# The first projection of a two-layer encoder trunk: the order of modulation and projection in the opening

## The chip, the cores and the metric

The kernel runs on one core of a Trainium2 chip, as one launch. The time is the device time of that launch, in microseconds (us). A core has a matrix engine (TensorE, PE in the rows; its weight loads are PEld), a vector engine (VectorE, DVE), an activation engine (ScalarE, ACT), GpSimd (POOL) and a queue engine (SyncE, SP). Each has its own list of instructions, and they wait for each other by semaphores. TensorE writes into eight banks of accumulator memory: `proj0`, `proj1`, `z0` to `z3`, `obank`, `misc`. Everything else lies in on-chip memory of 128 partitions, filled by DMA.

## The reference

The input x has 512 rows of 1024 values, c has 1024 values. What bears on the change is the start of layer 0:

```python
cond = jax.nn.silu(c)
mod = cond @ ada_w[l] + ada_b[l]
sh1, sc1, g1, sh2, sc2, g2 = jnp.split(mod, 6, axis=-1)
h = modulate(rms_norm(x, norm_mix_g[l]), sh1, sc1)     # h * (1 + scale) + shift
proj = h @ w_in                                        # 1024 x 2304 in layer 0
sq, sk, sv, wq, wk, wv = jnp.split(proj, cuts, axis=-1)
```

The projections feed stick-breaking attention (8 heads: logits, a log-sigmoid, a suffix sum over the keys, weights, values) and a sliding-window attention with sinks. Then come an output projection, a gated feed-forward net with a convolution, a second layer with a gated linear recurrence, and a last norm.

## The kernel before

A row of 1024 values is eight blocks of 128 (`DC = 8`). The activations lie transposed, block by block: `hT_hi[:, dc, :]` is block dc of the modulated input for all 512 rows. Each product is made of three matmuls in a faster number format: the value is split in a high part (`hi`, a copy by ScalarE) and the rest (`lo`, a subtraction by VectorE), and hi times hi, lo times hi and hi times lo are summed. A unit is one block of 128 output columns: 8 blocks x 3 = 24 matmuls of 512 columns. Its weights come into `w_raw`, ScalarE makes `w_hi` (`split`, L654), VectorE `w_lo` (L1068).

The list `STEPS0` orders layer 0 on all engines: `Q` is the opening group of four units, `u` a unit, `A` the logits of a head, `B` its suffix sums, `C` the values of two heads, `T` a transpose of values, `L` a window head. The lists of the engines are written out by hand in this order; nothing reorders them.

The opening, before the first `A`: SyncE loads x, then half of the shift and scale columns of `ada_w` (8 pieces of 512 KB, L512), the weights of the four units for the first four blocks (L522), the other half of the columns, the other weights. ScalarE sums the squares of x, scales its rows by the inverse root (L726), TensorE transposes them (L1867), ScalarE copies them as `x_hat` (L730). The rows of x are transposed without the factor too, for the residual `xT` (L1796, L752). VectorE multiplies each piece of the columns by its value of `cond` and adds it up over the 8 pieces (`first_block`, L1165, L1168). TensorE sums that over the partitions with a column of ones (`first_sums`), VectorE adds the bias and makes `scale_g` (`first_columns`, L1175, L1179). ScalarE makes the high part of the modulated block with scale and shift in one instruction (L738), and the block itself (L745); VectorE the low part (L1196). TensorE computes the four units SQ, SK, SV and WK for the first half of the blocks (`quad(0)`), and, after the second half of the columns, for the rest (`quad(1)`). Between its pieces of work it runs matmuls whose result nobody reads (`keep_clock`).

After `Q`, `A` 0 starts. `flip` (L1278) copies queries and keys to the other half of the partitions. For each head VectorE makes four sums (L1360) and four low parts (L1366), for which `B` waits. `ada_blocks` sums further modulation columns (L1208, L1211), `clear_queries` writes zeros (L1284, L1285).

## Time and profile before

| what | value |
|---|---|
| median of 3 runs | 1299.79 us (1299.79 to 1300.24) |
| the profiled execution, its own time | 1300.57 us |
| its span | 1298.8 us |
| TensorE busy | 1262.1 us, 97% |
| VectorE busy | 818.4 us, 63% |
| ScalarE busy | 554.8 us, 43% |
| chain that ended last | PE 88%, DVE 5%, queue of SP 2%, ACT 2%, DMA 1% |

The span is what the trace covers; the rest of the execution's own time lies around it. In the rows a line such as L1168 is a line of the kernel; an idle time in square brackets stands with what ended it. Where several matmuls stand in one row, the time runs from the start of the first to the end of the last. A matmul of full precision makes two records.

### The profile page before, as it was taken

What the parts mean: (1) busy time and instruction counts of PE and PEld (TensorE: products, weight loads), DVE (VectorE), ACT (ScalarE), POOL (GpSimd) and SP (SyncE); (2) the same over time, 40 slices, a digit from 0 to 9 for tenths busy, and PEclk for the clock granted to TensorE, in tenths of its full rate; (3) what the DMA queues carried; (4) which work ended last, traced back from release to release, by engine and by line L of the source; (5) the groups of instructions that cost most, each with busy time, mean ns of one, the idle gap of its engine ahead of it and who ended that gap; (6) DMA issues with size and microseconds to landing.
All of it is one profiled execution on the core that took longest, in us unless ns stands there. A gap on an engine that the chain in (4) does not pass through costs nothing.

```text
span 1298.8 us, 18991 instructions
## 1 busy us (share of the span) xinstructions
PE 1262.1 (97%) x7071; PEld 1021.7 (79%) x7071; DVE 818.4 (63%) x1191; ACT 554.8 (43%) x837; POOL 46.8 (4%) x92
## 2 busy tenths in 40 slices
PE   6999998999999999999999999999999999999997
PEld 5777777868888888878778888888688888888786
DVE  5776667676666666556787887776855555552423
ACT  7665556343333333121356655653433333331212
POOL 1000000000000000001000000001000000000000
PEclk9999999999999999999999999999999999999999
DMA  9644520535445454556513222226233333332232
GB/s 331 196 130 146 163 81 2 163 97 162 145 142 146 134 154 145 172 160 226 184 55 94 66 82 74 78 78 210 66 102 96 96 95 97 97 97 97 92 103 81
DMA packets 190074, 160.09 MB, mean 123 GB/s; under 512 B 5271, under 2 KB 163176, under 8 KB 190018
## 3 DMA queue, kind: packets, MB, share of 16 engines
q1 hardware_dynamic: 177696, 116.34, 29.7%
q0 software_dynamic: 11776, 42.29, 10.8%
q8 instruction: 38, 0.62, 0.2%
q10 hardware_dynamic: 546, 0.69, 0.1%
q14 instruction: 18, 0.15, 0.0%
HBM read 157.20 MB, written 2.10 MB: 123 GB/s over the span
## 4 chain that ended last, share of the span: by engine, by line
PE 88%; DVE 5%; SPq 2%; ACT 2%; issue 1%; DMA 1%; DVEq 0%; ACTq 0%
PE proj L1684 62%; PE z L1684 21%; PE obank L1684 3%; PE misc L1684 1%; SPq L512 1%; SPq L522 1%; DVE normed L1106 1%; DVE hT_lo L1112 1%; ACT w_hi L654 1%; DMA w_raw<-ab_w_in 1%; DVE w_lo L1068 0%; DVE xT L1491 0%; PE z L2244 0%; ACT hT_hi L686 0%; PE misc L1957 0%
## 5 line engine op out<-in xcount | busy, mean ns | idle before, releaser
L1684 PE MATMUL proj<-hT_hi,w_hi 128*128 128x512 f32 x1112 | 439.6, 396 | 1.1 <-ACT hT_hi L686 0.9
L1684 PE MATMUL proj<-hT_lo,w_hi 128*128 128x512 f32 x1112 | 434.6, 391 | 2.9 <-DVE hT_lo L1112 2.9
L1068 DVE TENSOR_TENSOR w_lo<-w_raw,w_hi 128x1024 fp32r<-128x1024 f32 x189 | 231.1, 1224 | 321.4 <-ACT w_hi L654 321.3
L1684 PE MATMUL proj<-hT_hi,w_lo 128*128 128x512 f32 x1112 | 433.2, 390 | 0.0
L654 ACT ACTIVATE w_hi<-w_raw 128x1024 fp32r<-128x1024 f32 x191 | 201.9, 1058 | 404.0 <-PE proj L1684 230.9
L1684 PEld LDWEIGHTS proj<-hT_lo,w_hi 128*128 128x128 f32 x1112 | 208.8, 188 | 52.4 <-DVE hT_lo L1112 9.3
L1684 PEld LDWEIGHTS proj<-hT_hi,w_hi 128*128 128x128 f32 x1112 | 208.8, 188 | 50.3 <-issue 8.7
L1684 PEld LDWEIGHTS proj<-hT_hi,w_lo 128*128 128x128 f32 x1112 | 208.7, 188 | 44.2
L1684 PE MATMUL z<-gated_hi,w_hi 128*128 (+1 forms) x264 | 103.6, 392 | 2.7 <-DVE xT L1491 2.7
L1684 PE MATMUL z<-gated_hi,w_lo 128*128 (+1 forms) x264 | 103.1, 390 | 0.0
L1684 PE MATMUL z<-gated_lo,w_hi 128*128 (+1 forms) x264 | 103.0, 390 | 0.0
L1211 DVE SCALAR_TENSOR_TENSOR ada_sum<-ada_raw,cond,ada_sum 128x1024 f32<-128x1024 f32 x70 | 89.6, 1280 | 2.8 <-DMA ada_raw<-ada_w 0.7
L906 ACT ACTIVATE square<-square,small 128x512 f32<-128x512 f32 x44 | 31.9, 724 | 133.8 <-DVE square L1454 133.8
L600 POOL DMA_DIRECT2D ada_raw<-ada_w x80 | 42.2, 528 | 843.4 <-DVE ada_sum L1211 439.2
L1684 PEld LDWEIGHTS z<-gated_hi,w_hi 128*128 128x128 f32 x264 | 49.6, 188 | 13.7 <-DVE xT L1491 3.1
L1684 PEld LDWEIGHTS z<-gated_hi,w_lo 128*128 128x128 f32 x264 | 49.7, 188 | 10.5
L1684 PEld LDWEIGHTS z<-gated_lo,w_hi 128*128 128x128 f32 x264 | 49.7, 188 | 10.0
L1461 DVE TENSOR_TENSOR h<-proj,square 128x512 f32<-128x512 f32 x44 | 30.4, 691 | 20.9 <-ACT square L906 20.0
L672 ACT ACTIVATE square<-xT 128x512 f32<-128x512 f32 x28 | 17.7, 632 | 51.5 <-DVE xT L1416 31.4
L1454 DVE SCALAR_TENSOR_TENSOR square<-normed,small,square 128x512 f32<-128x512 f32 x44 | 33.1, 752 | 6.6 <-DVE square L1450 5.8
L1684 PE MATMUL proj<-gated_hi,w_hi 128*128 (+1 forms) x88 | 35.2, 400 | 0.6 <-DVE w_lo L1068 0.6
L1450 DVE SCALAR_TENSOR_TENSOR square<-normed,small,square 128x512 f32<-128x512 f32 x44 | 33.1, 751 | 3.9 <-DVE square L1447 0.2
(342 smaller groups left out, 1485.5 us busy)
## 6 DMA issues: line engine op xcount, KB each, us to landing
ada_raw<-ada_w POOLq DMA_DIRECT2D x80, 512.0 KB, 4.2
w_raw<-ffn_w_gate SPq DMA_DIRECT2D x44, 512.0 KB, 3.8
w_raw<-ffn_w_up SPq DMA_DIRECT2D x44, 512.0 KB, 3.8
w_raw<-ffn_w_down SPq DMA_DIRECT2D x44, 512.0 KB, 3.3
w_raw<-hg_w_in SPq DMA_DIRECT2D x32, 512.0 KB, 4.1
ada_first<-ada_w SPq DMA_DIRECT2D x16, 512.0 KB, 11.0
w_raw<-ab_w_in SPq DMA_DIRECT2D x14, 512.0 KB, 4.0
w_raw<-ab_w_out SPq DMA_DIRECT2D x8, 512.0 KB, 4.2
```

The lines of the kernel that those rows point to most:

```text
L512: sp.dma_start(ada_first[:, DC * (1 - h) + k, :].rearrange("p (g n) -> p g n", g=2), src).then_inc(ada_first_in[h][k], 16)
L522: sp.dma_start(w_raw[:, p, i * 512:(i + 1) * 512].rearrange("p (k n) -> p k n", k=HALVES0), columns(rows, P * QUAD[2 * p + i])).then_inc(r ...
L600: pool.dma_start(ada_raw[:, m % ADA_SLOTS, :], ada_w[layer].rearrange("(p k) n -> p k n", k=DC)[:, k, which * D:(which + 1) * D]).then_inc ...
L654: nc.scalar.activation(dst, w_raw[:, slot, :], ACT.Copy).then_inc(hi_done, 1)
L672: nc.scalar.activation(dst, xT[:, dc, :], ACT.Square).then_inc(sq_done, 1)
L906: nc.scalar.activation(square[:, 1, :], square[:, 0, :], ACT.Gelu_apprx_tanh, bias=conv_col(layer, 3, f)).then_inc(gelu_done, 1)
L1068: nc.vector.tensor_tensor(w_lo[:, slot, :], w_raw[:, slot, :], w_hi[:, slot, :].bitcast(F32), ALU.subtract).then_inc(lo_done, 1)
L1211: nc.vector.scalar_tensor_tensor(out=acc, in0=raw, scalar=scale, in1=acc, op0=ALU.mult, op1=ALU.add).then_inc(ada_used, 1)
L1450: nc.vector.scalar_tensor_tensor(out=square[:, 0, :], in0=normed[:, 0, 1:1 + SEQ], scalar=conv_col(layer, 1, f), in1=square[:, 0, :], op0= ...
L1454: nc.vector.scalar_tensor_tensor(out=square[:, 0, :], in0=normed[:, 0, 2:2 + SEQ], scalar=conv_col(layer, 2, f), in1=square[:, 0, :], op0= ...
L1461: nc.vector.tensor_tensor(h32[:, 0, :], proj[1][:], square[:, 1, :], ALU.mult).then_inc(gp_done, 1)
L1684: return nc.tensor.matmul(dst, weights_ap, moving, start=start, stop=stop, skip_group_check=True)
```

## The change

The opening is put in another order. SyncE loads the weights of the four units in four pieces (a piece holds two blocks, for all four units) and between them the scale columns, for blocks 0 and 1, 2 and 3, 4 to 7; after them the shift columns, the weights of two single units, and the tables. The four units are SQ, SQ+1, SK and SK+1; SV and WK follow as single units after `A` 0.

The factors of the scale are summed by TensorE alone: per block and piece four matmuls with a weight of 128x32 and one moving column, `cond` (`scale_products`). The inverse root is spread over the partitions by TensorE (`diag`), and VectorE multiplies xT by it (`hat`). The four units are computed over x_hat times scale, without the shift. The shift is summed as before, by VectorE over 8 pieces (`shift_sums`); its part of the four units is a number per output column, made by 128 small matmuls from the raw weights (`quad_bias_of`) and added where the banks are copied out. The modulated input with the shift, which all later units need, is then made anew: `shifted_high` on ScalarE, `shifted_value` and `shifted_low` on VectorE, eight blocks. GpSimd makes the low weights of the units 4 and 5.

On VectorE, before, from the last block of the first half to the last one ahead of `A` 0 (`hT_lo` is a low part of the input, `ada_sum` the sums over the pieces, `quad_w` low weights):

```order
L1196 TENSOR_TENSOR hT_lo<-normed,hT_hi 128x512
L1168 SCALAR_TENSOR_TENSOR ada_sum<-ada_first,cond,ada_sum 128x1024 x5
L1074 TENSOR_TENSOR quad_w<-w_raw,quad_w 128x1024
L1175 TENSOR_TENSOR mod<-misc,small 128x2x4
L1179 SCALAR_TENSOR_TENSOR scale_g<-mod,small 128x4
L1190 TENSOR_SCALAR normed<-x_hat,scale_g,mod 128x512
L1196 TENSOR_TENSOR hT_lo<-normed,hT_hi 128x512
L1074 TENSOR_TENSOR quad_w<-w_raw,quad_w 128x1024
L1196 TENSOR_TENSOR hT_lo<-normed,hT_hi 128x512 x3
```

The same engine with the change, from the low part of block 4 to the first block with the shift:

```order
L1262 SCALAR_TENSOR_TENSOR hT_lo<-x_turn,scale_g,hT_hi 128x512
L1204 TENSOR_SCALAR ada_sum<-x_nat,cond 128x1024
L1207 SCALAR_TENSOR_TENSOR ada_sum<-x_nat,cond,ada_sum 128x1024
L1262 SCALAR_TENSOR_TENSOR hT_lo<-x_turn,scale_g,hT_hi 128x512
L1207 SCALAR_TENSOR_TENSOR ada_sum<-x_nat,cond,ada_sum 128x1024 x2
L1262 SCALAR_TENSOR_TENSOR hT_lo<-x_turn,scale_g,hT_hi 128x512
L1207 SCALAR_TENSOR_TENSOR ada_sum<-shift_low,cond,ada_sum 128x1024 x2
L1262 SCALAR_TENSOR_TENSOR hT_lo<-x_turn,scale_g,hT_hi 128x512
L1207 SCALAR_TENSOR_TENSOR ada_sum<-shift_low,cond,ada_sum 128x1024
L1207 SCALAR_TENSOR_TENSOR ada_sum<-ada_sum,cond 128x1024
L1235 TENSOR_TENSOR mod<-misc,small 128x8
L1269 TENSOR_SCALAR normed<-x_turn,scale_g,mod 128x512
```

The eight sums of the first half are gone, those that are left lie between the low parts of blocks 4 to 7, and the remade input begins behind them.

On VectorE around `A` 0, before (`k_sw` are window keys, `oT` and `h` the copies of `flip`):

```order
L1068 TENSOR_TENSOR w_lo<-w_raw,w_hi 128x1024 x2
L1328 COPY k_sw<-obank 64x512 x4
L1278 COPY oT<-q_sb 64x512 x2
L1278 COPY h<-k_sb 64x512 x2
L1360 SCALAR_TENSOR_TENSOR soft_a<-z,soft_a 128x128
```

With the change, from the copy of the second queries on (`normed` is a block with the shift):

```order
L1352 TENSOR_SCALAR q_sb<-proj,c_now 128x512
L1269 TENSOR_SCALAR normed<-x_turn,scale_g,mod 128x512
L1275 TENSOR_TENSOR hT_lo<-normed,hT_hi 128x512
L1269 TENSOR_SCALAR normed<-x_turn,scale_g,mod 128x512
L1275 TENSOR_TENSOR hT_lo<-normed,hT_hi 128x512
L1269 TENSOR_SCALAR normed<-x_turn,scale_g,mod 128x512
L1275 TENSOR_TENSOR hT_lo<-normed,hT_hi 128x512
L1358 TENSOR_SCALAR k_sb<-obank,c_now 128x512
L1269 TENSOR_SCALAR normed<-x_turn,scale_g,mod 128x512
L1275 TENSOR_TENSOR hT_lo<-normed,hT_hi 128x512
L1269 TENSOR_SCALAR normed<-x_turn,scale_g,mod 128x512
```

Seven more pairs of this kind and two copies stand ahead of the first `flip`; the window keys come after the first head's low parts.

On TensorE with the change, the columns of the scale (`cond,scale_...`) inside the blocks 1 and 3 of the four units:

```order
L1782 MATMUL z<-hT_hi,w_hi 128x512
L1782 MATMUL proj<-hT_hi,w_hi 128x512 x2
L1782 MATMUL obank<-hT_hi,w_hi 128x512
L1782 MATMUL z<-hT_hi,w_lo 128x512
L1782 MATMUL proj<-hT_hi,w_lo 128x512 x2
L1782 MATMUL obank<-hT_hi,w_lo 128x512
L1782 MATMUL z<-cond,scale_early 32x1 x64
L1782 MATMUL z<-hT_lo,w_hi 128x512
L1782 MATMUL proj<-hT_lo,w_hi 128x512 x2
...
L1782 MATMUL z<-cond,scale_late 32x1 x128
L1782 MATMUL z<-hT_lo,w_hi 128x512
L1782 MATMUL proj<-hT_lo,w_hi 128x512 x2
```

Block 1 ends behind 64 small matmuls and block 3 behind 128; before, 32 stood ahead of each half. The core of the diff:

```diff
-QUAD = [SQ, SK, SV, WK]
+QUAD = [SQ, SQ + 1, SK, SK + 1]
 STEPS0 = [
-    ("Q", 0), ("A", 0), ("T", 0), ("u", SQ + 1), ("B", 0), ("u", SK + 1),
+    ("Q", 0), ("A", 0), ("u", SV), ("u", WK), ("B", 0), ("T", 0),
...
+EARLY = len(QUAD) + 2
+PIECES = 4
+SCALES = [(0, 2, 0), (1, 2, 2), (2, 4, 4)]
...
+            def scale_load(i):
+                at, n, dc = SCALES[i]
+                for j in range(DC // 2):
+                    sp.dma_start(scale_raw[i][:, 2 * j:2 * j + 2, :],
+                                 first_ada[:, 2 * j:2 * j + 2, 1, dc * P:(dc + n) * P]
+                                 ).then_inc(scale_in[i][j * len(scale_in[i]) // 4], 16)
+
+            def shift_load(k):
+                sp.dma_start(shift_raw[k], first_ada[:, k, 0, :]).then_inc(shift_in[k // 2], 16)
...
             quad_load(0)
...
+            scale_load(0)
             quad_load(1)
+            scale_load(1)
+            quad_load(2)
+            scale_load(2)
+            quad_load(3)
+            sp.wait_ge(xt_full, DC)
+            for k in range(4):
+                shift_load(k)
+            unit_load(4)
             sp.dma_start(table2, tables[:, 2 * P:9 * P]).then_inc(bands_in, 16)
...
+            for k in range(4, DC):
+                shift_load(k)
+            unit_load(5)
+
...
+            def early_split(u):
+                pool.wait_ge(hi_done, u + 1)
+                nc.gpsimd.tensor_tensor(w_lo[:, u % 2, :], w_raw[:, u % 2, :], w_hi[:, u % 2, :].bitcast(F32),
+                                        ALU.subtract).then_inc(early_low, 1)
+
+            for u in range(len(QUAD), EARLY):
+                early_split(u)
+
+            pool.wait_ge(misc_full, MISC_AT["bias1"] + 1)
...
+            def first_high(dc):
+
+                act.wait_ge(hat_first, dc + 1)
+                act.wait_ge(first_mods, min(dc // 2, 2) + 1)
+                nc.scalar.activation(hT_hi[:, dc, :], x_hat(dc), ACT.Copy, scale=scale_g[:, 0, dc:dc + 1]
+                                     ).then_inc(h_hi, 1)
...
+            act.wait_ge(spread_full, 2)
+            nc.scalar.activation(x_rstd[:], zb[2][:], ACT.Copy).then_inc(spread_done, 1)
+            x_rows(4)
+            first_high(0)
+            first_high(1)
+            x_rows(5)
+            x_rows(6)
+            x_rows(7)
+            quad_high(1)
+            first_high(2)
+            first_high(3)
+            quad_high(2)
+            first_high(4)
+            first_high(5)
+            quad_high(3)
+            first_high(6)
+            first_high(7)
+            split(4, 0)
...
+            def shifted_high(dc):
+
+                if dc == 0:
+                    act.wait_ge(misc_free, MISC_AT["shift"] + 1)
+                    act.wait_ge(unit_mm, len(QUAD))
+                nc.scalar.activation(hT_hi[:, dc, :], x_hat(dc), ACT.Identity, scale=scale_g[:, 0, dc:dc + 1],
+                                     bias=mod[:, 0, dc:dc + 1]).then_inc(fix_hi, 1)
...
             def first_low(dc):
...
                 dve.wait_ge(h_hi, dc + 1)
+                nc.vector.scalar_tensor_tensor(out=hT_lo[:, dc, :], in0=x_hat(dc), scalar=scale_g[:, 0, dc:dc + 1],
+                                               in1=hT_hi[:, dc, :].bitcast(F32), op0=ALU.mult, op1=ALU.subtract
+                                               ).then_inc(h_lo, 1)
+
+            def shifted_value(dc):
+                if dc > 1:
+                    dve.wait_ge(fix_lo, dc - 1)
+                nc.vector.tensor_scalar(normed[:, dc % 2, 2:2 + SEQ], x_hat(dc), scale_g[:, 0, dc:dc + 1],
+                                        mod[:, 0, dc:dc + 1], ALU.mult, ALU.add).then_inc(shifted, 1)
+
+            def shifted_low(dc):
+                dve.wait_ge(shifted, dc + 1)
+                dve.wait_ge(fix_hi, dc + 1)
                 nc.vector.tensor_tensor(hT_lo[:, dc, :], normed[:, dc % 2, 2:2 + SEQ], hT_hi[:, dc, :].bitcast(F32),
...
+                                        ALU.subtract).then_inc(fix_lo, 1)
...
                     ada_block(*divmod(j, DC))
                 ada_next[0] += n
 
...
+            for dc in range(3):
+                x_rows(dc)
+            dve.wait_ge(x_root, 1)
+            for i in range(TB):
+                nc.vector.tensor_scalar(diag[:, i, :], ident, sumsq[:, 16 + i:17 + i], None, ALU.mult
+                                        ).then_inc(diag_ready, 1)
+            x_rows(3)
+            hat(0)
             dve.wait_ge(misc_free, MISC_AT["small"] + 1)
+            scale_columns(0)
+            hat(1)
+            quad_split(0)
+            first_low(0)
+            first_low(1)
...
+            hat(2)
             quad_split(1)
...
+            scale_columns(1)
+            hat(3)
+            first_low(2)
+            hat(4)
+            quad_split(2)
+            first_low(3)
+            hat(5)
+            hat(6)
+            scale_columns(2)
+            hat(7)
+            quad_split(3)
+            for dc in range(4, DC):
                 first_low(dc)
...
+                shift_sums(2 * dc - 8)
+                shift_sums(2 * dc - 7)
+            shift_columns()
+            dve.wait_ge(unit_mm, len(QUAD))
+            dve.wait_ge(misc_free, MISC_AT["shift"] + 1)
+            shifted_value(0)
+            bias_columns(0)
+            shifted_low(0)
+            bias_columns(1)
+            dve.wait_ge(misc_free, MISC_AT["bias1"] + 1)
+            nc.vector.tensor_scalar(q_sb[:, 1, :], quad_banks[1][:], HEAD ** -0.5, quad_bias[:, 2:3], ALU.mult, ALU.add
+                                    ).then_inc(quad_out[1], 1)
+            for dc in range(1, DC):
+                shifted_value(dc)
+                shifted_low(dc)
+                if dc == 3:
+                    nc.vector.tensor_scalar(k_sb[:, 1, :], quad_banks[3][:], quad_bias[:, 3:4], None, ALU.add
+                                            ).then_inc(quad_out[3], 1)
...
+            def scale_products(i):
+
+                _, n, dc = SCALES[i]
+                for k in range(DC):
...
+                    for c in range(n):
+                        for row in range(0, P, QUADRANT):
+                            last = mm(column_bank[f"scale{i}"][row:row + QUADRANT, c:c + 1],
+                                      scale_raw[i][:, k, c * P + row:c * P + row + QUADRANT], cond[:, 2, k:k + 1],
+                                      start=k == 0 and c == 0)
...
+            def quad_bias_of(name, units):
+                for n, i in enumerate(units):
+                    for dc in range(DC):
+                        w = weights_at(quad_raw, i, dc)
+                        for row in range(0, P, QUADRANT):
+                            last = mm(column_bank[name][row:row + QUADRANT, n:n + 1], w[:, row:row + QUADRANT],
+                                      mod[:, 0, dc:dc + 1], start=n == 0 and dc == 0)
+                last.then_inc(misc_full, 1)
...
+            def quad_block(dc):
+
+                c = dc // 2
...
                 pe.wait_ge(h_hi, dc + 1)
...
+                pe.wait_ge(quad_low, c + 1)
+                for i in range(4):
+                    mm(quad_banks[i][:], weights_at(quad_lo, i, dc), hT_hi[:, dc, :])
+                if dc == 1:
+                    pe.wait_ge(x_new, X_BASE)
+                    scale_products(1)
+                if dc == 3:
+                    scale_products(2)
...
+                    last = mm(quad_banks[i][:], weights_at(quad_hi, i, dc), hT_lo[:, dc, :], stop=(dc == DC - 1))
...
+            keep_clock(obank, 3)
+            for i in range(TB):
+                pe.wait_ge(x_in[i], 16)
+            for dc in range(6):
+                x_columns(dc)
...
+            pe.wait_ge(diag_ready, TB)
...
+                last = mm(obank[:, i * P:(i + 1) * P], ones, diag[:, i, :], True, True)
+            last.then_inc(spread_full, 1)
+            pe.wait_ge(x_early, 3)
+            for i in range(TB):
+                last = mm(zb[2][:, i * P:(i + 1) * P], ones, diag[:, i, :], True, True)
+            last.then_inc(spread_full, 1)
+            for dc in range(6, DC):
+                x_columns(dc)
+            pe.wait_ge(x_early, X_BASE)
+            pe.wait_ge(cond_ready, 1)
+            misc_wait("scale0")
+            scale_products(0)
+            pe.wait_ge(x_new, X_BASE - 1)
+            pe.wait_ge(hat_first, 2)
+            keep_clock(zb[3], 2)
+
+            def quad_units():
+                for dc in range(DC):
+                    quad_block(dc)
+                pe.wait_ge(first_used, DC)
+                column_sums("shift", ada_sum[:, 1, :], DC)
+                pe.wait_ge(misc_free, MISC_AT["shift"] + 1)
+                quad_bias_of("bias0", (0, 2))
+                quad_bias_of("bias1", (1, 3))
...
-                    unit(u, u % 2, proj[u % 2][:], mod_group=MOD_IN_UNIT0.get(b))
+                    unit(u, u % 2, proj[u % 2][:], fix_lo if u == len(QUAD) else None, MOD_IN_UNIT0.get(b))
```

## Rows read from the trace of the kernel before

**Rows 1.** The longest pieces of the chain that ended last, 0 to 120 us: start, us, engine, line
```profile
57.25 2.75 PE z L1684 x12
...
60.58 5.46 PE proj L1684 x24
...
81.86 3.01 PE z L1684 x20
```

**Rows 2.** Stretches of 2 us: length, busy us of each engine, clock, DMA share, GB/s
```profile
16.00:18.00 2.00, 1.78 (x13) 1.34 (x12) 1.79 (x3) 1.19 (x2) 0.00 (x0) 1.00 1.05 388
22.00:24.00 2.00, 2.00 (x71) 1.44 (x70) 1.19 (x2) 0.51 (x1) 0.00 (x0) 1.00 1.20 290
42.00:44.00 2.00, 1.14 (x8) 0.84 (x8) 0.55 (x1) 2.00 (x4) 0.00 (x0) 1.00 0.44 113
44.00:46.00 2.00, 1.79 (x5) 1.46 (x6) 1.74 (x2) 2.00 (x4) 0.00 (x0) 0.66 0.50 149
```

**Rows 3.** TensorE in order of time: start us, us, engine, line, operation, form, count
```profile
10.22 6.56 PE L1684 MATMUL z<-slope_r,ident_r 128*128 128x512 f32 x20
...
20.52 1.47 PE L1796 MATMUL z<-table,x_nat 128*128 128x128 f32 x12
...
23.32 0.71 PE L1684 MATMUL misc<-table,ada_sum 128*32 128x1 f32 x64
...
45.32 0.63 PE L1684 MATMUL obank<-hT_hi,quad_w 128*128 128x512 f32 x1
45.74 0.63 PE L1684 MATMUL z<-hT_lo,quad_w 128*128 128x512 f32 x1
...
57.57 2.42 PE L1684 MATMUL z<-q_sb,k_sb 64*128 64x128 f32 x8
```

**Rows 4.** ScalarE in order of time, 0 to 100 us
```profile
10.94 1.05 ACT L699 ACTIVATE ada_sum<-x_nat 128x1024 f32<-128x1024 f32 x1
...
26.21 0.80 ACT L738 ACTIVATE hT_hi<-x_hat,mod,scale_g 128x512 fp32r<-128x512 f32 x1
...
31.67 1.55 ACT L752 ACTIVATE xT<-z 128x512 f32<-128x512 f32 x3
39.37 1.06 ACT L654 ACTIVATE quad_w<-w_raw 128x1024 fp32r<-128x1024 f32 x1 [6.15 <-DMA w_raw<-ab_w_in]
```

**Rows 5.** VectorE in order of time, the opening up to the first attention head
```profile
30.12 1.28 DVE L1168 SCALAR_TENSOR_TENSOR ada_sum<-ada_first,cond,ada_sum 128x1024 f32<-128x1024 f32 x1
31.32 0.69 DVE L1196 TENSOR_TENSOR hT_lo<-normed,hT_hi 128x512 fp32r<-128x512 f32 x1
...
33.72 6.84 DVE L1168 SCALAR_TENSOR_TENSOR ada_sum<-ada_first,cond,ada_sum 128x1024 f32<-128x1024 f32 x5
...
41.60 0.16 DVE L1175 TENSOR_TENSOR mod<-misc,small 128x8 f32<-128x8 f32 x1
...
42.10 0.55 DVE L1190 TENSOR_SCALAR normed<-x_hat,scale_g,mod 128x512 f32<-128x512 f32 x1
```

**Rows 6.** VectorE in order of time, the first and second attention head
```profile
50.78 0.40 DVE L1263 TENSOR_REDUCE ada_sum<-table 128x32 f32<-128x128 f32 x1
...
57.28 2.80 DVE L1328 COPY k_sw<-obank 64x512 f32<-64x512 f32 x4 [3.83 <-PE obank L1684]
60.00 0.87 DVE L1278 COPY oT<-q_sb 64x512 f32<-64x512 f32 x2
...
63.28 1.68 DVE L1360 SCALAR_TENSOR_TENSOR soft_a<-z,soft_a 128x128 f32<-128x128 f32 x4 [1.50 <-ACT soft_a L828]
64.88 1.69 DVE L1366 TENSOR_TENSOR softplus<-soft_a,softplus 128x128 fp32r<-128x128 f32 x4
...
68.55 1.22 DVE L1068 TENSOR_TENSOR w_lo<-w_raw,w_hi 128x1024 fp32r<-128x1024 f32 x1
69.93 0.48 DVE L1284 MEMSET q_sw<- 64x512 f32 x1 [0.16 <-issue]
```

**Rows 7.** GpSimd in order of time, its one compute instruction of the opening
```profile
0.75 0.53 POOL L604 MEMSET rstd<- 128x512 f32 x1 [0.29 <-POOLq L2272]
```

More of the change, by code:

```diff
@@ L1337, in _ @@
                         src = proj[u % 2]
-                        if b == WV:
+                        if b == WK:
+                            for g in range(2):
+                                for half in range(2):
+                                    last = nc.vector.tensor_copy(k_sw[HEAD * half:HEAD * half + HEAD, g, :],
+                                                                 src[HEAD * g:HEAD * g + HEAD, :])
+                            last.then_inc(proj_free[u % 2], 1)
+                        elif b == WV:
                             dve.wait_ge(misc_full, MISC_AT["V0"] + 1)
@@ new lines, in quad_block, with keep_clock @@
+                    if dc == DC - 1:
+                        last.then_inc(unit_mm, 1)
+                if dc % 2 and dc < DC - 1:
+                    last.then_inc(quad_part, 1)
+            def keep_clock(dst, n):
+                for _ in range(n):
+                    mm(dst[:], ident_r[:], slope_r[:, 0:4, :].rearrange("p a n -> p (a n)"), True, True)
+            pe.wait_ge(table_in, 16)
+            pe.wait_ge(tables_ready, SW_HEADS)
+            keep_clock(obank, 3)
+            for i in range(TB):
+                pe.wait_ge(x_in[i], 16)
```

390 lines of the change are left out of this document (154 added, 236 removed).

## The prediction

> **What bounds the kernel now.** I read the chain that ended last first, then the stretches, then the three engines in order of time. From `A` 0 on the chain is TensorE almost without a break: `A` 0 from 57.25, a unit of 24 matmuls in 5.46 us (0.228 each), the suffix sums of head 1 at 81.86 [rows 1]. So what the opening gives or takes reaches the end, if nothing behind it waits anew. In the opening it is the DMA: ScalarE sat 6.15 us before the weights of the second half came [rows 4], at 388 GB/s for wide rows of memory and 290 for narrow ones [rows 2]. The change removes that wait, since half of the columns now come behind the four units. The question is whether VectorE and the small pieces of work, one behind the other, are ready when the data is.
>
> **The change, part by part.** All of it is counted on the profiled execution (1300.57 us).
>
> *Up to the first factors.* The last block of x is there at about 10.9 [rows 4]. TensorE is slow then: the twenty clock matmuls from 10.22 took 6.56 us where twenty at 0.23 take 4.6 [rows 3], so it ran at its lower level (0.42 a matmul, as between 45.32 and 45.74 [rows 3]) until about 14. 24 transposes, 0.11 each at full speed (twelve in 1.47 [rows 3]) and twice that before 14: until 15.1; four small ones: 15.5. The spread of the root is eight matmuls of full precision with 128 columns; queries and keys take 2.42 for 1280 columns [rows 3], so 0.22 each: 17.2. Eight transposes: 18.1. The columns of blocks 0 and 1 are 64 small matmuls. The 64 records of 32 such matmuls took 0.71, or 0.02 a matmul [rows 3]: 1.3, with three clock matmuls 2.1, so 20.2. The way back through VectorE takes 0.5 (from 41.60 to 42.10 [rows 5]), then two factors on ScalarE at 0.7 apart (0.80 is the row with scale and shift [rows 4]) and three copies of xT at 0.48 (three in 1.55 [rows 4]), for which TensorE waits: the second copy has ended at 23.1.
>
> *The four units.* Two clock matmuls, then block 0 and two thirds of block 1, 20 matmuls at 0.235: 28.3. 64 column matmuls: 29.6. Now the same way again: 0.5 on VectorE, 0.8 for a factor: 31.0. Block 2 and two thirds of block 3: 35.7. 128 column matmuls: 38.3. VectorE: 38.8. Two factors and one high weight (1.06 [rows 4]) on ScalarE: 41.2. The low weight on VectorE, a subtraction as in [rows 6] with 1.22: 42.4. None of this waits for a DMA: it comes to about 6 MiB behind x, 6.3 MB, there at 27 with 388 GB/s and at 33 with 290 throughout [rows 2].
>
> *The shift.* VectorE has four low parts left, about 0.65 each (0.60 to the next for the subtraction of 0.69 [rows 5]; the new form multiplies too), and eight sums: the first is a plain product, about 0.8 to the next; a sum takes 1.28, 1.20 to the next if that is another operation [rows 5], 1.39 if it is a sum on the same tile (five in 6.84 [rows 5]). 2.6 + 2.0 + 3 x 2.6 = 12.4: the last sum ends at 54.8. The shift columns have long landed: 10.4 MiB behind x until the last of them, 10.9 MB, are there at 39 with 388 GB/s, at 48.5 with 290.
>
> *To `A` 0.* From the last sum to the columns on VectorE it was 1.04 before (40.56 to 41.60 [rows 5]): 55.8. ScalarE makes two shifted blocks (0.80 each [rows 4]) while TensorE makes 64 of the 128 bias products; then the bias goes through VectorE, and queries and keys are copied, 0.6 each: `A` 0 at about 59.0, where it was 57.1 by the rows (57.57 less the half microsecond of its masks [rows 3]). That is **+1.9**. The bands are ready: their table landed before the last shift rows.
>
> *Behind `A` 0.* Here lies most of the loss. From 59.0 on VectorE has, without a pause: a copy of the second queries (0.6), seven blocks with the shift and their low parts (0.55 [rows 5], 0.61 and 0.60 to the next: 8.5), the second keys (0.6); three small ones and the small reduction (0.40 [rows 6]), 1.1; `flip` 1.7 (0.87 twice [rows 6]); sums and low parts of head 0, 3.4 [rows 6]; two blocks of columns, 2.0 (0.75 estimated as half a sum and a little, 1.28 [rows 5]); two low weights, 2.3 [rows 6]; the window keys 2.5 (2.80 with their tail [rows 6]); eight times zeros, 0.48 and 0.16 apart [rows 6]: 5.1; `flip` of head 2, 1.7; sums of head 1 and its first low part, 2.0. That is 31.5 us: `B` 1 can start at 90.4. It started at 81.86 [rows 1]. Before, the window keys and `flip` were done in the shadow of `A` 0, and the remade blocks did not exist. TensorE itself would be through unit WV at about 85.7 (59.0, plus 2.4, unit SV held by the remade blocks until 69.3, WK 5.5, `B` 0 and `T` 0 3.2, `A` 1 1.9, WV 5.5): it stands nearly 5 us. That is **+8.5** in place of the 1.9, and behind it the lists are those of before, so it stays.
>
> *TensorE's clock.* Before, TensorE was busy 1.14 of the 2 us from 42.00, with eight transposes, and the next stretches were granted 0.66 and less [rows 2]: 0.42 a matmul, about nine of them, 1.7 us lost. With the change there are two such places on the path: the wait up to 23.1, behind small matmuls, and the 5 us before `B` 1. Bounds 0 and 3.4 together; I take **2.5**, near the upper end, since the row before shows the loss for a shorter pause. The Trainium skill ("TensorE: Matmul & The Clock Gate", What's actually happening) says the slow clock is the default and activity releases it; the trace agrees with its 0.66. If small column matmuls counted as activity in full, the sum would lack the first 1.7.
>
> *GpSimd.* Two low weights for SV and WK. The subtraction of the same size takes 1.22 on VectorE [rows 6], the only compute row of GpSimd is 0.53 for half the size [rows 7]; 1.1 to, with a factor of four, 5 each. Cover is large: they start at about 43.5 and unit SV at 61.4. Their own time costs nothing.
>
> Sum: 8.5 + 2.5 = +11.0, 1311.6 by the profiled execution; the median shown is 0.8 lower, 1310.8. I say **1311**.
>
> **The rivals.** *VectorE is held up by GpSimd.* The two subtractions fall at 43.5 to 48.5, in the middle of VectorE's eight sums, which are on the path. If the two engines exclude each other for an instruction, the sums end later by at least 2 x 1.22: 1314, more if GpSimd is slower. No row shows the two at once. "SBUF — State Buffer", Who interferes with whom, of the Trainium skill has it so: a VectorE instruction with two inputs in SBUF and a GpSimd instruction that reads SBUF block each other whole. "GPSIMD Engine Reference", Elementwise — side-by-side cycle accounting, has 1.96 times VectorE's time, which makes an estimate of 2 x 2.4 and 1316. With it goes the case that the column matmuls are slower at the lower clock (192 on the path, 0.02 more each would be +3.8: 1315).
>
> *The other side: faster.* If the factors were through by 28, as the scale columns land, the sums of the shift would follow the landings, the last at 39 to 40.6: last sum 43.3, `A` 0 at 47.5, and VectorE's list of 31.5 ends at 79.0, 2.9 before the 81.86: 1297.7. For it the landings speak; against it stand two trips over TensorE, VectorE and ScalarE of 9 us each (20.2 to 29.6, 29.6 to 38.8), which hang on one another and on no DMA. It decides at scale factors for blocks 4 to 7 by about 33: earlier than that is faster, later slower.
>
> *No difference.* The +1.9 at `A` 0 stays, and VectorE's list is made up in its shadow: 1302.5. It takes the 5 us that TensorE stands before `B` 1 to vanish, so 6 us less on VectorE than counted from rows.
>
> **The numbers.** Forecast (1305 to 1313): 0.58. Held up by GpSimd or slow columns (1313 to 1318): 0.30. No difference 0.06, faster 0.06. The range leaves the last two and the far end out: 1304 to 1317. By 0.2% (2.6 us, about what a measurement of this kernel tells from no change): faster 0.06, same 0.06, slower 0.88.
>
> **What would show it.** Right: `A` 0 at 58 to 62; VectorE with two waits for TensorE's columns before about 29.7 and 38.4; the last shift sum at 54 to 60, without a wait for DMA; TensorE idle 4 to 6 us before the suffix sums of head 1, released by VectorE's low parts; granted clock below 1 near 22 to 26 and behind that idle time; the same durations from `A` 2 on. Wrong: an `A` 0 near 48, shift sums that wait for `ada_w`, or no idle time before `B` 1. A VectorE instruction of 2 us or more in the middle of the sums would show the first rival.

## The result and the profile after

The changed kernel takes **1328.50 us** (median of 4, 1328.13 to 1329.66) where the kernel before takes 1300.01 beside it: ratio 1.0219, 95% interval 1.0207 to 1.0231. The forecast was 1311 (1304 to 1317): right in sign, 17.5 us short. TensorE is busy 1276.5 us for 1262.1, and its mean granted clock is 0.982 for 0.997. The page has the clock by fortieths of the span:

```profile
PEclk8779999999999999999999999999999999999999
```

The kernel before has a 9 in all forty places; the first digits here, 8 7 7, are the first 100 us, and there the clock was lower. Four stretches of 4 us of the changed kernel, columns as in [rows 2] (length; busy us of TensorE, its weight loads, VectorE, ScalarE, GpSimd; clock, DMA share, GB/s):

```profile
24.00:28.00 4.00, 3.49 (x8) 2.84 (x9) 3.02 (x5) 1.89 (x3) 0.00 (x0) 0.50 1.07 378
40.00:44.00 4.00, 1.41 (x139) 1.28 (x130) 0.00 (x0) 0.00 (x0) 0.00 (x0) 0.77 0.58 188
52.00:56.00 4.00, 0.92 (x4) 0.39 (x3) 4.00 (x2) 0.00 (x0) 4.00 (x2) 0.98 0.46 132
...
76.00:80.00 4.00, 4.00 (x8) 1.70 (x7) 3.90 (x8) 1.31 (x5) 0.02 (x1) 0.50 0.94 355
```

From 40 to 44 no engine but TensorE works, and that one only 1.41 us of the 4. From 52 to 56 VectorE is busy all the time with two instructions, and GpSimd too. Then the rows of TensorE, which answer to [rows 1, 3]:

```profile
31.61 1.25 PE L1782 MATMUL z<-cond,scale_early 128*32 128x1 f32 x128
38.98 1.11 PE L1782 MATMUL z<-cond,scale_late 128*32 128x1 f32 x113
41.22 1.31 PE L1782 MATMUL z<-cond,scale_late 128*32 128x1 f32 x128 [1.12 <-issue]
44.68 0.39 PE L1782 MATMUL z<-cond,scale_late 128*32 128x1 f32 x15 [2.15 <-issue]
...
70.14 0.22 PE L1782 MATMUL z<-mod,ada_sum 128*32 128x1 f32 x3 [1.86 <-issue]
...
73.59 0.28 PE L1782 MATMUL z<-mod,ada_sum 128*32 128x1 f32 x5 [1.57 <-issue]
74.28 1.08 PE L1782 MATMUL z<-table_r,ident_r 128*128 128x128 f32 x4 [0.42 <-DVE c_now L1243]
75.30 4.63 PE L1782 MATMUL z<-q_sb,k_sb 64*128 64x128 f32 x8
92.39 2.93 PE L1782 MATMUL z<-softplus,table_r 128*128 128x128 f32 x20
106.53 4.59 PE L1782 MATMUL z<-softplus,table_r 128*128 128x128 f32 x20 [3.02 <-DVE softplus L1464]
121.39 2.94 PE L1782 MATMUL z<-softplus,table_r 128*128 128x128 f32 x20
```

The idle times inside one run of the same small matmuls wait for nothing that the rows of TensorE show ("issue"). The DMA rows show something: from 66 to 76 us, where hardly anything else moves, the queue that loads instructions (`q8`) brought two packets, 0.03 MB in all. The 40 slices of this stretch, 0.25 us each, have them at about 67.5 and 71.2; the pauses end at 70.14 and 73.59. From 36 to 48 us there are two as well. For which engine they are the rows do not say.

```profile
GB/s 0 0 0 0 0 33 66 0 0 0 0 0 0 0 0 0 0 0 0 0 66 0 0 0 0 0 0 0 0 0 0 0 0 0 0 0 0 82 164 49
q8 instruction: 2, 0.03, 1.3%
```

`A` 0 begins at 74.28 (57.1 before), its eight logits take 4.63 us (2.42 in [rows 3]), `B` 1 stands at 106.53 (81.86 in [rows 1]). VectorE and GpSimd, which answer to [rows 5]:

```profile
50.56 3.25 DVE L1207 SCALAR_TENSOR_TENSOR ada_sum<-x_nat,cond,ada_sum 128x1024 f32<-128x1024 f32 x1
53.73 2.82 DVE L1262 SCALAR_TENSOR_TENSOR hT_lo<-x_turn,scale_g,hT_hi 128x512 fp32r<-128x512 f32 x1
...
64.35 1.28 DVE L1207 SCALAR_TENSOR_TENSOR ada_sum<-ada_sum,cond 128x1024 f32<-128x1024 f32 x1
```
```profile
50.13 5.87 POOL L653 TENSOR_TENSOR w_lo<-w_raw,w_hi 128x1024 fp32r<-128x1024 f32 x2 [45.24 <-ACT w_hi L690]
```

A sum that takes 1.28 us takes 3.25, and a low part of 0.75 takes 2.82, while GpSimd makes its two low weights: 1.97 and 2.07, 4.0 together.

### The profile page after: what moved, and what is told of

Read it like the earlier page. It is cut to its first block, busy times and chain, and to the rows that moved or that the text cites. A ratio compares the mean times of both kernels' runs of the same rounds, so it can differ in the third digit from the quotient of the medians.

```text
span 1326.6 us, 20362 instructions
## 1 busy us (share of the span) xinstructions
PE 1276.5 (96%) x7734; PEld 1032.7 (78%) x7734; DVE 829.3 (63%) x1219; ACT 546.0 (41%) x823; POOL 52.9 (4%) x94
## 4 chain that ended last, share of the span: by engine, by line
PE 88%; DVE 7%; ACT 2%; issue 2%; DMA 1%; SPq 0%; DVEq 0%; ACTq 0%
PE proj L1782 60%; PE z L1782 22%; PE obank L1782 3%; PE misc L1782 2%; DVE normed L1147 1%; ACT w_hi L690 1%; DVE hT_lo L1153 1%; DMA x_nat<-x 1%; DVE w_lo L1114 0%; PE z L1900 0%; DVE xT L1589 0%; DVE hT_lo L1262 0%; DVE ada_sum L1207 0%; PE z L2364 0%; ACT hT_hi L722 0%
## 5 line engine op out<-in xcount | busy, mean ns | idle before, releaser
L708 ACT ACTIVATE square<-xT 128x512 f32<-128x512 f32 x28 | 17.7, 632 | 51.5 <-DVE xT L1514 31.4
```

What stands on the lines that cost most here:

```text
L708: nc.scalar.activation(dst, xT[:, dc, :], ACT.Square).then_inc(sq_done, 1)
```

## The experiments

Every kernel is the changed one with the edit shown, unless the text names another; of longer edits the core is shown, and line numbers are shifted by a few; "dc" is a block. A time is the median of 4 runs (one run for `e6_twice`), the change against 1329.0, the middle of the changed kernel's two medians.

**GpSimd later** (`e1_low_later`).

```diff
                 pool.wait_ge(hi_done, u + 1)
+                pool.wait_ge(first_used, DC)
```

> GpSimd makes its two low weights only after the last shift sum, instead of in the middle of the sums. Theory (GpSimd holds VectorE up): the sum of 3.25 us and the low part of 2.82 us go back to 1.28 and 0.75, so the last sum ends 4.0 us sooner (65.6 to 61.6), TensorE's pause of 3.69 us before the low part of block 5 is gone, A 0 is 4 to 5 us earlier and the whole 1328.5 - 4.5 = 1324 us (1323 to 1326). Rival (those two were slow because of the transfers of weights in the same microseconds): the durations and the time stay, 1328.5.

1326.07: -3.0. VectorE and GpSimd:

```profile
51.84 1.28 DVE L1208 SCALAR_TENSOR_TENSOR ada_sum<-x_nat,cond,ada_sum 128x1024 f32<-128x1024 f32 x1
53.04 0.75 DVE L1263 SCALAR_TENSOR_TENSOR hT_lo<-x_turn,scale_g,hT_hi 128x512 fp32r<-128x512 f32 x1
...
61.58 1.28 DVE L1208 SCALAR_TENSOR_TENSOR ada_sum<-ada_sum,cond 128x1024 f32<-128x1024 f32 x1
```
```profile
63.02 4.85 POOL L654 TENSOR_TENSOR w_lo<-w_raw,w_hi 128x1024 fp32r<-128x1024 f32 x2 [58.11 <-DVE ada_sum L1208]
```

Both durations are back, and from the scale columns on VectorE (46.41, 45.13 in the changed kernel) to the end of the last sum it is 16.4 us instead of 20.5: the 4.0 expected. The rest of the time went into an opening that was 1.3 us later on that occasion. The Trainium skill ("SBUF — State Buffer", Who interferes with whom) has it that a VectorE instruction with two inputs in on-chip memory and a GpSimd instruction that reads it exclude each other; the trace of the changed kernel agrees, for whole instructions: GpSimd's first subtraction starts at 50.13, and with its 2.43 us and the 1.28 of the sum behind it that makes 53.84, where the sum ended at 53.81. The estimate of 2.4 us for GpSimd's subtraction is right too: 4.85 for two.

**A quarter of the instructions** (`e2_full_columns`), for the columns of the last scale piece and of the bias:

```diff
+                        if i == 2:
+                            last = mm(column_bank["scale2"][:, c:c + 1], scale_raw[i][:, k, c * P:(c + 1) * P],
+                                      cond[:, 2, k:k + 1], start=k == 0 and c == 0)
+                            continue
...
-                        for row in range(0, P, QUADRANT):
-                            last = mm(column_bank[name][row:row + QUADRANT, n:n + 1], w[:, row:row + QUADRANT],
-                                      mod[:, 0, dc:dc + 1], start=n == 0 and dc == 0)
+                        last = mm(column_bank[name][:, n:n + 1], w, mod[:, 0, dc:dc + 1], start=n == 0 and dc == 0)
```

> The scale columns of blocks 4 to 7 and the bias columns are made with weights of 128x128, one matmul where there were four of 128x32: a quarter of the instructions, the same products. Theory (TensorE runs out of instructions: three stretches of about 128 pairs of weight load and matmul each took 3.46 us, pause included): the pauses of 1.12 and 2.15 us at 40 to 44.7 and of 1.86 and 1.57 at 68.3 to 73.6 are gone; 32 matmuls cost 0.11 each by the transposes, 3.5 us for the 5.9 and 3.5 for the 6.5: -5.4, 1323 us (1321 to 1325). Rival (the pauses are waits for data or for a bank, or come from the slow clock): they stay where they are, and the wider weights cost 1 to 2 us more: 1330.

1338.60: +9.6. The columns of the scale on TensorE and the stretches from 40 to 44 and 44 to 48:

```profile
40.11 10.28 PE L1782 MATMUL z<-cond,scale_late 128*128 128x1 f32 x64
```
```profile
40.00:44.00 4.00, 4.00 (x37) 3.96 (x35) 0.00 (x1) 0.00 (x0) 0.00 (x0) 0.98 0.60 190
44.00:48.00 4.00, 4.00 (x20) 4.00 (x20) 0.00 (x0) 0.00 (x0) 0.00 (x0) 0.50 0.01 2
```

The pauses are gone, as the theory of instructions says, but the price was wrong: a pair with 128 columns of weight takes 0.11 us at full clock (37 in 4 us) and 0.20 at half (20 in 4 us), where four with 32 take 0.04. I had also counted one such time for a matmul that is two pairs. And the clock is at 0.50 in a stretch in which TensorE is busy without a gap.

**Sums sooner** (`e3_sums_sooner`).

```diff
             hat(6)
+            for k in range(4):
+                shift_sums(k)
             scale_columns(2)
```

> VectorE makes the first four shift sums before it waits for the scale columns of blocks 4 to 7, in the 6.3 us in which it stood. Theory (the end of the sums sets A 0, and only their place in the list kept them from the idle time): 4.6 us of sums leave the list behind 45.1, the last ends at 61, A 0 comes 4.5 us sooner, 1324 us (1323 to 1326). Rival (the shift rows are not there yet, by landings of 12.3 us after the first issue at 19.7 some are only just): the scale columns wait for the sums and nothing is won, 1328 to 1331.

1325.58: -3.4. From the scale columns to the last sum it is 15.7 us for 20.5, so the rows had landed and VectorE's place in the list was the limit.

**Zeros later** (`e4_zeros_later`).

```diff
-                elif kind == "B" and b == 0:
+                elif kind == "B" and b == 1:
                     clear_queries()
```

> The eight zero fills of the window queries (5.1 us on VectorE, behind the low parts of head 0) go behind the low parts of head 1. Theory (VectorE's list behind A 0, 31.5 us as forecast and 31.6 as measured, sets B 1): VectorE is ready 5.1 us sooner, TensorE's pause of 4.1 us before the suffix sums of head 1 is gone, with it the slow clock behind it: 1328.5 - 4.1 - 1.0 = 1323.4 us (1322 to 1325). Rival (the fills are then in the way of head 2, or TensorE waits for something else there): 1327 to 1329.

1325.97: -3.0. The suffix sums of heads 0 to 2:

```profile
94.08 2.93 PE L1782 MATMUL z<-softplus,table_r 128*128 128x128 f32 x20
105.03 2.93 PE L1782 MATMUL z<-softplus,table_r 128*128 128x128 f32 x20
119.36 3.04 PE L1782 MATMUL z<-softplus,table_r 128*128 128x128 f32 x20 [0.93 <-DVE softplus L1464]
```

`B` 1 is 10.95 us behind `B` 0 instead of 14.14, without a pause. The pause had been 3.0 us, not the 4.1 that I had read; another of 0.93 stands a head later, behind the zeros.

**Again** (`e0_again`), the changed kernel unaltered, on the chip of the next three.

> The changed kernel itself once more, beside the others: the first four experiments all showed an opening 0.7 to 1.2 us later than the one profile of the changed kernel (block 0 at 26.2 to 26.7 for 25.5), ahead of anything they changed. If that is scatter from run to run, the median here is 1328 to 1330 and block 0 of this profile may lie anywhere from 25.5 to 26.7; if it is the chip, the time is 1329 to 1331 and block 0 at 26.5.

1329.58, block 0 at 26.11: scatter of about a microsecond in the opening, and what the experiments are compared with.

**Scale on VectorE** (`e5_scale_vector`).

```diff
...
             quad_split(1)
+            for k in range(DC):
+                if k % 2 == 0:
+                    dve.wait_ge(scale_in[2][k // 2], 16)
+                sums(scale_late[:, k, :], ada_sum[:, 0, 0:4 * P], 0, k)
             scale_columns(1)
...
-                if dc == 3:
-                    scale_products(2)
+                if dc == 2:
+                    pe.wait_ge(first_used, DC)
+                    column_sums("scale2", ada_sum[:, 0, :], 4)
...
```

> One part undone: the scale of blocks 4 to 7 is summed by VectorE again (eight sums of 512 columns, in the 5.8 us in which it stood between 27.1 and 32.9; the rows landed by 28.4), and TensorE makes 32 pairs of weight load and matmul in place of 256, in block 2. Theory (the 256 pairs, with the pauses in them, are on the path): the columns stop costing TensorE 6 us, the factors of blocks 4 to 7 come at 39 instead of 45.3, the last shift sum at 59.5, A 0 at 69: -6, 1322.5 us (1321 to 1325). Rival (VectorE is the scarce engine, and the sums push its factors of blocks 2 and 3 back): not under 1327.

1322.84: -6.2, the largest single effect. VectorE at its scale sums and columns:

```profile
27.80 5.68 DVE L1207 SCALAR_TENSOR_TENSOR ada_sum<-scale_late,cond,ada_sum 128x512 f32<-128x512 f32 x7
...
39.17 0.15 DVE L1226 TENSOR_TENSOR mod<-z,small 128x4 f32<-128x4 f32 x1
```

The factors come at 39.2 for 45.1, without a wait, and the last sum ends at 59.6 for 65.6. The first sums still take 3.24 and 2.82 us beside GpSimd, so this effect and that of `e1_low_later` are separate.

**Shift ahead of the bias** (`e7_shift_first`).

```diff
...
-            shifted_value(0)
-            bias_columns(0)
-            shifted_low(0)
-            bias_columns(1)
+            for dc in range(3):
+                shifted_value(dc)
+                shifted_low(dc)
+            bias_columns(0)
+            shifted_value(3)
+            shifted_low(3)
+            bias_columns(1)
...
```

ScalarE's blocks 2 and 3 are moved in the same way.

> VectorE and ScalarE make the shifted blocks 0 to 3 while TensorE makes the bias columns, in place of waiting for them; the copies of queries and keys with the bias come behind. Theory (VectorE's list from the bias to the suffix sums of head 1 sets B 1, A 0 does not): of the 5.4 us in which VectorE waited for the bias columns 3.5 are filled, A 0 stays where it is within 1 us and B 1 comes 3.5 us sooner: 1325 us (1323.5 to 1326.5). Rival (A 0 itself sets B 1, by its logarithms on ScalarE): 1328 to 1330.

1329.05: nothing. VectorE's low weight for the third unit behind `A` 0 (93.74, after 0.56 idle, in the changed kernel), and TensorE:

```profile
94.36 1.23 DVE L1116 TENSOR_TENSOR w_lo<-w_raw,w_hi 128x1024 fp32r<-128x1024 f32 x1 [4.00 <-ACT w_hi L690]
```
```profile
93.01 2.93 PE L1787 MATMUL z<-softplus,table_r 128*128 128x128 f32 x20
107.14 4.59 PE L1787 MATMUL z<-softplus,table_r 128*128 128x128 f32 x20 [3.02 <-DVE softplus L1469]
```

VectorE was 2.8 us ahead at the sums of head 0 and gave it all back in waiting 4.00 us for a high weight, which itself waits for TensorE to be through unit WK. My theory fell: shortening VectorE's list ahead of that wait does not move `B` 1. TensorE's stream from `A` 0 to the end of WK sets it, and behind that only the last 14.14 us of the list.

**All of them** (`e8_all`): scale on VectorE, GpSimd later, zeros later, shift ahead.

> All at once: GpSimd's low weights behind the sums (4.0 in the trace), scale of blocks 4 to 7 on VectorE (6), shifted blocks ahead of the bias (3.5), zero fills later (3.0), and TensorE's pause before B 1 with its slow clock gone (1.5). Theory (these are separate pieces of one path): 1328.5 - 16 to 18 = 1311 to 1313 us, still slower than before, since VectorE has 28 us between A 0 and B 1 where it had 24. Rival (they overlap, one hides behind the other): 1316 to 1322.

1315.93: -13.1. The single effects add to 12.2 (3.0 + 3.0 + 6.2 + 0), within the microsecond of scatter, so they are separate pieces; the expectation was too high by about the 3.5 of the shift. This is the best kernel tried with the whole computation, and still 1.3% slower than before (ratio 1.0129, 1.0112 to 1.0146). GpSimd now hits the shifted block, 1.69 us for 0.55 though it reads one tile alone, and its low part, 2.73 for 0.69:

```profile
56.40 1.69 DVE L1272 TENSOR_SCALAR normed<-x_turn,scale_g,mod 128x512 f32<-128x512 f32 x1
58.12 2.73 DVE L1278 TENSOR_TENSOR hT_lo<-normed,hT_hi 128x512 fp32r<-128x512 f32 x1
```

**Twice the small matmuls** (`e6_twice`): `scale_products(2)` makes its loop twice.

> The 128 small matmuls of the scale of blocks 4 to 7 are made twice over (the second pass writes the same columns anew), 512 pairs of weight load and matmul in a row for 256. Theory (TensorE gets no more than 128 pairs in 3.46 us, whatever they are): from the first small matmul to the last 6.3 + 6.9 = 13.2 us, with a pause behind each 128 pairs, and the whole 6.9 us longer than the changed kernel, 1336. Rival (the pauses belong to one place, a wait that the rows do not name): the second pass costs its execution alone, 256 x 0.010 = 2.6 us, 1332.

One run, 1337.03: +8.0. TensorE:

```profile
38.37 1.11 PE L1782 MATMUL z<-cond,scale_late 128*32 128x1 f32 x113
40.60 1.23 PE L1782 MATMUL z<-cond,scale_late 128*32 128x1 f32 x128 [1.12 <-issue]
44.88 1.88 PE L1782 MATMUL z<-cond,scale_late 128*32 128x1 f32 x128 [3.05 <-issue]
48.89 1.89 PE L1782 MATMUL z<-cond,scale_late 128*32 128x1 f32 x128 [2.13 <-issue]
52.63 0.39 PE L1782 MATMUL z<-cond,scale_late 128*32 128x1 f32 x15 [1.85 <-issue]
```

A pause behind every 128 pairs, one start to the next 4.28, 4.01, 3.74 us (3.46 in the changed kernel); from first to last 14.65 us for 6.1. A wait of one place is excluded: in a long run TensorE gets no more than 128 pairs in 3.5 to 4.3 us here. The Trainium skill ("Advanced Engine Details and Errata", ISA Cache) has cache lines of 256 instructions, which are 128 pairs; the trace agrees with the step.

**Clock matmuls in the opening** (`e9_keep_opening`).

```diff
             scale_products(0)
+            keep_clock(zb[3], 10)
```

> Ten clock matmuls behind the scale columns of blocks 0 and 1, in the 3 us in which TensorE stands before block 0. Theory (the pause and the small matmuls ahead of it bring the clock to its lower level, and block 0 and half of block 1 are on the path): block 0 starts where it did and its eight matmuls at 0.43 become 0.23, -1.6 us; the time 1328.9 - 1.6 = 1327.3 (1326.5 to 1328.3). Rival (block 0's slow matmuls are hidden, since block 1 waits for its factor anyway): no change.

1329.19: nothing. TensorE behind them:

```profile
33.04 0.40 PE L1782 MATMUL z<-hT_lo,w_hi 128*128 128x512 f32 x1 [1.08 <-issue]
...
34.26 1.05 PE L1782 MATMUL proj<-hT_hi,w_hi 128*128 128x512 f32 x2
...
40.24 2.10 PE L1782 MATMUL z<-cond,scale_late 128*32 128x1 f32 x231
45.05 0.51 PE L1782 MATMUL z<-cond,scale_late 128*32 128x1 f32 x25 [2.71 <-issue]
```

Blocks 0 and 1 ran at full clock: from block 0 (26.06) to the second columns 4.65 us for 6.1 to 6.3. From these columns to the next it took 9.5 us for 7.4: the clock fell in block 2, and behind the 128 pairs TensorE stood for 1.08 us ("issue"), which it did not in the changed kernel. From block 0 to the end of the last columns it is 19.5 us in both, so what the clock gave ahead of the columns was taken back there. The result is the rival's, its reason is not. The pauses also do not come at a fixed count: here 231 pairs came in a row before the second one.

**Clock matmuls in the bias** (`e10_keep_bias`), on top of all four edits.

```diff
                                       mod[:, 0, dc:dc + 1], start=n == 0 and dc == 0)
+                        if dc % 2:
+                            keep_clock(zb[2], 1)
```

> All the edits of before (1315.9 us), and 16 clock matmuls between the small ones of the bias, where TensorE stands for instructions anyway. Theory (on the path from A 0 to the unit WK is TensorE, at 0.43 a matmul for its first 8 us, because the bias left the clock low): the bias takes no longer (6.9 us for 256 pairs by supply, 2.7 + 3.8 by execution), A 0 goes from 4.6 us to 2.4 and seven matmuls behind it from 0.43 to 0.23: -3.6, 1312.3 us (1311 to 1314). Rival (the clock matmuls lengthen the bias by their own 3.8 us, as VectorE waits for it): 1315 to 1317.

1323.04: +7.1 on the 1315.93. At the start of the bias on TensorE:

```profile
55.70 0.31 PE L1792 MATMUL z<-mod,ada_raw 128*32 128x1 f32 x16 [0.29 <-DVE mod L1238]
55.94 0.49 PE L1792 MATMUL z<-slope_r,ident_r 128*128 128x512 f32 x1
```

16 pairs with one clock matmul take 0.66 us at full clock (the clock matmuls start at 55.94, 56.60, 57.26) and 1.05 at half, not the 0.4 that I added up, and from the fourth on the clock is down though TensorE never stood (from 60 to 68 it is busy 8.00 of 8.00 us at a clock of 0.50).

**Both** (`e11_all_keep`).

> Both sets of clock matmuls and all the edits of before. Theory (separate pieces of the path): 1312.3 - 1.6 = 1310.7 us (1309 to 1313), still 10 us above the kernel before. Rival (the ten in the opening bring nothing here, because VectorE's eight sums of the scale, which wait for no TensorE, set the factors of blocks 2 to 7): as the kernel with the bias edit alone, 1312.

1323.86, as the kernel with the bias edit: clock matmuls in the opening are worth nothing here either.

**A short bias** (`e12_short_bias`), seven of eight parts of the bias products left out: `for dc in range(1)` for `range(DC)`.

> The changed kernel with only the first of the eight blocks in the bias sums (32 pairs of weight load and matmul for 256, so the queries and keys are not the reference's). Theory (two bounds lie within 0.6 us of one another at B 0: VectorE's list from the shift columns on, and TensorE's stream at the slow clock): A 0 is 6.5 us sooner and takes 2.4 us for 4.6, TensorE has 9 us in hand, but VectorE's list gives only its 5.4 us of waiting back: B 1 is 5 us sooner, and no longer 14.14 behind B 0. 1328.9 - 5 = 1324 us (1322.5 to 1325.5). Rival (TensorE's stream alone sets B 1, as the constant 14.14 says): -9 to -10, 1319 to 1320.

1324.02: -5.0, as expected, but by the rival's mechanism and with half of its size. TensorE:

```profile
69.95 1.09 PE L1782 MATMUL z<-table_r,ident_r 128*128 128x128 f32 x4 [2.47 <-ACT k_sb L841]
...
88.07 2.93 PE L1782 MATMUL z<-softplus,table_r 128*128 128x128 f32 x20
```

The clock stayed down in `A` 0 (its logits take 4.63 us again) and `B` 1 is again 14.14 behind `B` 0: TensorE sets it, 4.3 us sooner because `A` 0 is.

**The same with all edits** (`e13_all_short_bias`).

> The same in the kernel with all edits (1315.9 us; there the zero fills stand later and the shifted blocks ahead of the bias). Theory (there TensorE's stream sets B 0 and B 1, with VectorE 2 to 4 us ahead of it): A 0 is 7 us sooner and at full clock, then VectorE's list binds after 6 us: B 1 at 87.5 for 93.6, 1310 us (1308.5 to 1311.5). Rival (the clock is low behind the short pieces whatever their number, and A 0 stays at 4.6 us): 1312 to 1313.

1315.42: -0.5 on the 1315.93, within the scatter, and neither theory. TensorE stood 8.20 us ahead of `A` 0, for the bias columns on VectorE, which the shifted blocks, drawn out by GpSimd, had pushed to 64. Putting the shifted blocks ahead gains nothing where the bias is short.

**A short bias with the clock kept** (`e14_short_bias_keep`): `keep_clock(zb[2], 10)` behind the short bias.

> The kernel with the short bias (1324.0 us; seven of eight parts of the bias products are left out) and ten clock matmuls behind the bias, in the 2.47 us in which TensorE stood there. Theory (TensorE's stream at the lower clock sets B 0, and VectorE has only 1.6 us in hand): the logits of head 0 take 2.4 us for 4.6, the matmuls behind them 0.23 for 0.43, B 0 comes up to 3.7 us sooner, B 1 by 1.6 and is then more than 14.14 behind B 0, for VectorE's list binds: 1322.4 us (1321.5 to 1323.3). Rival (the clock falls all the same, as it did among the clock matmuls in the bias): no gain, 1324 to 1326.

1322.89: -1.1. TensorE:

```profile
70.03 2.42 PE L1782 MATMUL z<-q_sb,k_sb 64*128 64x128 f32 x8
84.34 2.93 PE L1782 MATMUL z<-softplus,table_r 128*128 128x128 f32 x20
100.04 5.49 PE L1782 MATMUL z<-softplus,table_r 128*128 128x128 f32 x20 [4.59 <-DVE softplus L1464]
```

`A` 0 is at full clock and `B` 0 is 3.7 us sooner, but `B` 1 only 2.2, now 15.7 behind: VectorE's list binds. The longer pause before `B` 1 costs the clock behind it 1.5 us more (`B` 2 16.3 behind `B` 1 for 14.9). So with the short bias the slow clock at `A` 0 costs some 2 us at `B` 1, and 1.1 in the whole time. In the changed kernel itself VectorE had only 0.56 us in hand, so there it should cost less; that was not tried.

## Why the prediction was wrong

Up to `A` 0 it was right in order and wrong in four sizes; my times against the trace's:

| piece | forecast | measured | more |
|---|---|---|---|
| start to the scale columns of blocks 4 to 7 | 35.7 | 38.98 | 3.3 |
| these columns | 2.6 | 6.1 | 3.5 |
| from there to the end of the last shift sum | 16.5 | 20.6 | 4.1 |
| from there to `A` 0 | 4.2 | 8.65 | 4.4 |
| `A` 0 to `B` 1 | 31.4 | 32.25 | 0.9 |

These add to 16.1 us (but for rounding): `B` 1 at 106.5 for 90.4. Behind it came 3.1 for my 2.5. That makes the 16.8 between the forecast for the profiled execution and its time (1311.6 and 1328.39); the rest of the 17.5 is between the medians.

- **Column matmuls at 0.02 each** was the step that failed most (3.5, and most of the 4.4). I took the price from 64 records in a row [rows 3], which come out of what TensorE has at hand; 256 in a row don't. The execution was as priced; the pauses are 1.12 and 2.15 us in the columns of the scale and 1.86 and 1.57 in the bias, 6.7 together. Shown by `e2_full_columns` (pauses gone with a quarter of the instructions), `e6_twice` (more pauses with more) and `e5_scale_vector` (-6.2 without them). The rival "slow columns" had 3.8 for it, but by the clock, which is not the reason.
- **VectorE held up by GpSimd** was a rival at 0.30 together with the slow columns, with at least 2.4 us; it came true with 4.0 (`e1_low_later`). The two rivals were not alternatives: both prices were paid on top of the forecast, and their sum lies outside the range.
- **Up to the late columns** (3.3): the first columns end at 21.5 for 20.2, 1.3 later; from there through VectorE and ScalarE to block 0 it was 0.6 longer (25.5 for 23.6); and block 0 and part of block 1 ran at the lower clock, 1.4 more. I had put this last into the 2.5 for the clock.
- **The bias** (4.4): 3.4 are the two pauses of before. The other 1.0 is an omission: I let 64 products run beside ScalarE's blocks and forgot that `A` 0 waits for both halves of the bias, 128 matmuls, or 256 pairs. With 32 pairs in their place (`e12_short_bias`) it was 3.96 us from the last shift sum to `A` 0, for the 8.65 and my 4.2.
- **VectorE's list of 31.5 us** looks exact (32.25) and is half an accident. It was without a wait but for 0.56 us, yet TensorE's stream to the end of WK was as long: `B` 0 came 18.1 us behind `A` 0 where I had 15.8, since the clock was low there. With 2.8 us less on the list nothing was won (`e7_shift_first`). The loss behind `A` 0 itself was as forecast: 32.25 us for the 24.8 of before, 7.5 more where I had 6.6.
- **The clock, 2.5**: I had it low at two places. It was low at five: by the granted clock near 24 to 28, 44 to 48, 56 to 62, 70 to 83 and behind `B` 1. The second and third lie beside VectorE's sums, which were later than TensorE. Behind `B` 1 the distance to the kernel before grew by 3.1. `B` 2 is 14.9 behind `B` 1 for 13.3 before (the suffix sums at 106.53 take 4.59 for [rows 1] 3.01). The other 1.6 came at the window heads, 130 us later, where the instructions are the same. First the suffix sums of head 2 and the window heads before, then the window heads with the change:

```profile
95.18 2.94 PE L1684 MATMUL z<-softplus,table_r 128*128 128x128 f32 x20
...
216.85 0.98 PE L1919 MATMUL proj<-table,q_sb 128*128 128x128 f32 x7 [2.46 <-DVE q_sb L1309]
...
274.86 0.50 PE L1684 MATMUL proj<-hT_lo,w_hi 128*128 128x512 f32 x1 [0.48 <-DVE hT_lo L1112]
```
```profile
243.07 1.33 PE L2039 MATMUL proj<-table,q_sb 128*128 128x128 f32 x7 [2.46 <-DVE q_sb L1411]
...
302.67 0.50 PE L1782 MATMUL proj<-hT_lo,w_hi 128*128 128x512 f32 x1 [0.49 <-DVE hT_lo L1153]
```

26.2 us late at the first, 27.8 at the second, with the same pause of 2.46 ahead. The granted clock fell there in one kernel and not in the other (0.91 from 240 to 260, 1.00 from 220 to 240 before). Why is open; it was not tried. From there to the end the distance stays.

Right were: the sign, no wait for a DMA in the shift sums, and two waits of VectorE for columns (5.78 and 6.34 us, until 32.9 and 45.1 for my 29.7 and 38.4). The pause before the suffix sums of head 1 was there, released by VectorE's low parts, but with 3.02 us shorter than the 4 to 6 that I had (my own terms for TensorE's stream add to 85.4, not 85.7), because that stream was longer too. The sign of the first rival, a VectorE instruction of over 2 us in the middle of the sums, was there twice. That "faster" needed the late factors by 33 no run tested: they came at 45, and at 39 in `e5_scale_vector`, both slower.

## What to carry to other kernels

Price small instructions by how many stand in a row, not by one record: here TensorE waited for instructions behind 113 to 231 pairs of weight load and matmul, and the DMA rows show a load of instructions shortly before the ends of the pauses. Before giving GpSimd a share of VectorE's work, look for what VectorE does in those microseconds; here 4.9 us of help made two instructions on the path 4.0 longer, and moving it gave 3.0 of the whole time. When a list of one engine explains a distance exactly, look whether a second engine's stream ends there too: shorten one and see whether anything moves. And rivals that can hold together belong in the range as a sum.
